# Four norms by column halves, the entries and the ending by tile, and a down projection moved behind its up projection, in a two-block transformer kernel

## The chip, the core and the metric

The kernel runs on one core of a Trainium2 chip. The metric is the device time of one execution in microseconds. One core has five engines with instruction streams of their own: TensorE (PE, matmul), VectorE (DVE), ScalarE (ACT), GpSimd (POOL) and SyncE (SP). They meet only at semaphores, and each follows its stream in order. Matmuls accumulate in eight PSUM banks of 128 x 512 fp32.

## What is computed

512 tokens of 1024 fp32 features pass through two blocks, each followed by a normalization with `final_g`. The part of the reference that matters here, cut:

```python
# block one
x = x + merged @ w_mix_out                                   # site mx
hc = rmsnorm(x, norm_cross_g); x = x + cross_attention(...)  # site co
hf = rmsnorm(x, norm_ffn_g)
x = x + peer_ffn(hf, ...)      # per token 8 heads x 16 experts of 16384:
                               # gelu(hf . u_e) * g_e * v_e, summed over the 128 chosen
x = rmsnorm(x, final_g)        # "fa"
# block two
h = rms_norm(x, ...)           # mix2
y = concat(nsa_mixer, gmlp, conv); x = x + norm(y) @ w_ou    # site ou
x = x + cross_attention(rms_norm(x), ...)                    # site xo
x = x + conv_gated_ffn(rms_norm(x), w_up, w_down)            # up, down; D_FF = 2816
return rms_norm(x, final_g)    # "fb"
```

## The kernel before

The tokens are four tiles of 128; a half `h` is two tiles (`h=0`: tiles 0 and 1, `h=1`: tiles 2 and 3). `X` holds the residual of all four. Weights come in chunks of 128 x 1024 fp32 (512 KB) through a ring of six buffers, `RING`: SP issues the chunk with number k once PE has used the one with number k-6. Each expert is one indirect gather on POOL of 1 MB (a row of u and of v for each of 128 tokens) into one of eight slots. For each of the 512 gathers DVE makes a dot product (L1951), ACT the gelu and the gate (L1446, L1450), and the gated v row is added to X either by DVE (`add` on DVE, L1928) or by PE with a diagonal matrix into PSUM (L1180), whose sum DVE adds to X in `total` (L1941).

The order of all work is a list of steps that the class `Plan` writes; every engine, the DMA issue of SP among them, works off the steps that concern it in that order. The list has three stretches:

- `first_a`: block one of tiles 0 and 1 up to the norm `("ffn", 0)`.
- the weave: `weave(work, peers, choices)` interleaves three lists by the costs written beside the steps. `peers` are the 512 experts, tile by tile; `work` holds everything else of block one of tiles 2 and 3 and then `second(0, True)`, block two of tiles 0 and 1, up to its up projection `proj_T("up", 0, 11)`. While `light` is set, two of three experts are summed on PE.
- `second(1, False)`: block two of tiles 2 and 3. It starts when the experts of tile 3 are summed (`total` 3): final norm `fa` (`final_in` loads the gain row, `final_sq`, `final_inv`, `final_root`, `final_out`), norm `mix2`, eight transposes on each tile, the projections qn, kn, vn, zg, zc, `cmp1`/`cmp2`, 20 steps of attention (`nsa`: logits "nl" L1123, transposes "nt" L1088 and L1090, values "nv" L1102 and L1108), the y norm, ou, cross attention, up and down.

The down projection of tiles 0 and 1 stands inside `second(1)` (`late_down`): it runs over the 22 chunks of w_down twice, once for each tile, and its 44 pieces are placed by `beside(n)`: 8 before the mix2 transposes, 1 or 2 behind each attention step, the rest before the y transposes. Its matmuls (`down`, L1153) need nothing of tiles 2 and 3. `last(0)` (the final norm and the store of tiles 0 and 1) stands behind the ou projection and before the norm `("x", 2, 1)`.

A norm is: squares of both tiles with a row sum on ACT (`norm_sq`, L1228), mean and reciprocal on DVE (`norm_inv`, L1601, L1603), root on ACT (`norm_root`, L1233, with the load of the function table for it), scaling of one tile on ACT and of the other on DVE (`norm_out`, L1250, L1613), then 16 transposes on PE (L897, L898), evicted by ACT and DVE (L1259, L1627). `proj_T` (L909, L910) and `proj_tok` (L929, L930) are the two forms of a projection; `out_tok` adds its result to X by column halves of 512 (`residual`, L1638).

## Time and profile before

| | us |
|---|---|
| three runs | 2905.11, 2905.76, 2908.76 (median 2905.76) |
| the profiled execution | 2902.87 |
| its span in the trace | 2901.1 |
| PE busy | 2408.7 (83%) |
| DVE busy | 1765.4 (61%) |
| ACT busy | 1124.4 (39%) |
| POOL busy | 665.2 (23%) |

The profiled execution is 2.9 us below the median of the three runs, and 1.8 us longer than its span. Times in the rows are counted from the start of the span. A share of busy time is a mean over stretches that are bounded by different things, so each stretch is read by itself.

### The profile page before, as it was taken

How to read it: one execution, taken by the hardware profiler on the slowest of the kernel's cores; microseconds unless marked ns; L12 is line 12 of the kernel's file. 1: busy time of each engine (PE TensorE's matmuls, PEld its weight loads, DVE VectorE, ACT ScalarE, POOL GpSimd, SP SyncE). 2: the span in 40 equal slices, each digit the busy share in tenths (PEclk: the TensorE clock that was granted, in tenths of full speed). 3: DMA queues.
4: the chain of work that ended last, by engine and by line, in shares of the span. 5: the costliest groups of instructions: out<-in, count | busy, mean ns of one | idle time of the engine just before them, and what ended most of it. 6: DMA issues, size and time to landing. Idle time of an engine off the chain costs nothing.

```text
span 2901.1 us, 31007 instructions
## 1 busy us (share of the span) xinstructions
PE 2408.7 (83%) x10834; PEld 1655.5 (57%) x10834; DVE 1765.4 (61%) x4230; ACT 1124.4 (39%) x2762; POOL 665.2 (23%) x569
## 2 busy tenths in 40 slices
PE   8999999879978649778958588577984799988998
PEld 7786666657744327536626434354762376655873
DVE  2101311598797778676999898888998417312430
ACT  2101311242533764354442578464554225412210
POOL 0000000122343344332233334443234102100000
PEclk9999999989989879999979566699996699999999
DMA  6555343589999999999889989999999653443443
GB/s 205 173 153 166 96 145 126 213 333 371 403 412 417 416 392 391 419 398 393 314 333 416 368 324 379 390 419 419 416 418 419 258 161 111 152 131 94 153 153 116
DMA packets 160972, 838.74 MB, mean 289 GB/s; under 512 B 17400, under 2 KB 21896, under 8 KB 95024
## 3 DMA queue, kind: packets, MB, share of 16 engines
q0 software_dynamic: 73728, 536.90, 45.8%
q1 hardware_dynamic: 82464, 287.75, 28.6%
q10 hardware_dynamic: 4624, 12.11, 1.2%
q8 instruction: 86, 1.41, 0.2%
q14 instruction: 70, 0.57, 0.1%
HBM read 828.27 MB, written 8.41 MB: 288 GB/s over the span
## 4 chain that ended last, share of the span: by engine, by line
PE 50%; DVE 22%; ACT 13%; DMA 10%; issue 4%; POOL 0%; ACTq 0%; DVEq 0%; SPq 0%
PE ps L909 24%; DMA BIG<-in_uv,BIG 9%; DVE BIG L1951 6%; PE ps L929 5%; DVE X L1928 5%; PE ps L930 5%; PE ps L1153 5%; PE ps L910 3%; ACT L1446 2%; PE ps L1180 2%; DVE BIG L1859 1%; DVE BIG L1856 1%; PE ps L1123 1%; PE ps L1102 1%; ACT WK L1228 1%
## 5 line engine op out<-in xcount | busy, mean ns | idle before, releaser
L2168 POOL DMA_INDIRECT BIG<-in_uv,BIG x512 | 622.0, 1215 | 1635.1 <-DVE X L1928 576.0
L909 PE MATMUL ps<-BIG,RING 128*128 128x256 f32 x3472 | 810.6, 386 | 15.2 <-DMA RING<-in_w_cq 4.9
L909 PEld LDWEIGHTS ps<-BIG,RING 128*128 128x128 f32 x3472 | 665.5, 193 | 148.0 <-issue 26.5
L1951 DVE CUSTOM_DVE_ANT_0 BIG<-BIG 128x1024 f32<-128x1024 f32 x512 | 619.2, 1217 | 87.1 <-DMA BIG<-in_uv,BIG 84.8
L1928 DVE SCALAR_TENSOR_TENSOR X<-BIG,small,X 128x1024 f32<-128x1024 f32 x333 | 426.3, 1280 | 75.0 <-ACT small L1450 74.3
L1446 ACT ACTIVATE small<-small 128x1 f32<-128x1 f32 x512 | 102.7, 201 | 640.5 <-DVE small L1951 636.3
L909 PE MATMUL ps<-WK,RING 128*128 128x256 f32 x1232 | 291.0, 389 | 21.3 <-DVE BIG L1707 19.3
L909 PEld LDWEIGHTS ps<-WK,RING 128*128 128x128 f32 x1232 | 238.6, 195 | 62.2 <-DVE BIG L1707 26.8
L929 PE MATMUL ps<-RING,BIG 128*128 128x512 f32 (+1 forms) x448 | 225.7, 585 | 5.6 <-DVE BIG L1686 2.4
L930 PE MATMUL ps<-RING,BIG 128*128 128x512 f32 (+1 forms) x448 | 223.5, 580 | 0.0
L1279 ACT ACTIVATE BIG<-ps 128x256 f32<-128x256 f32 (+2 forms) x143 | 56.5, 397 | 375.8 <-PE ps L910 316.7
L1180 PE MATMUL ps<-BIG,DG 64*64 64x512 f32 x728 | 131.4, 811 | 82.3 <-ACT DG L1458 82.3
L1180 PE MATMUL ps<-BIG 64*64 64x512 f32 x704 | 126.8, 811 | 54.2 <-ACT BIG L1458 54.0
L1645 DVE TENSOR_SCALAR BIG<-ps 128x256 f32<-128x256 f32 (+2 forms) x37 | 16.8, 454 | 252.1 <-PE ps L910 207.7
L1153 PE MATMUL ps<-RING,BIG 128*128 128x512 f32 x352 | 161.3, 612 | 3.1 <-DVE X L1941 3.1
L897 PE MATMUL ps<-ident,BIG 128*128 128x128 f32 x128 | 48.0, 385 | 134.9 <-ACT BIG L1250 77.9
L1446 ACT ACT_TABLE_LOAD x117 | 150.1, 1283 | 2.7 <-issue 0.6
L1638 DVE TENSOR_TENSOR X<-ps,X 128x512 f32<-128x512 f32 x40 | 27.4, 690 | 198.2 <-PE ps L930 117.9
L910 PE MATMUL ps<-BIG,RING 128*128 128x256 f32 x496 | 147.5, 379 | 0.0
L929 PEld LDWEIGHTS ps<-RING,BIG 128*128 128x128 f32 x448 | 84.1, 191 | 106.6 <-issue 93.9
L930 PEld LDWEIGHTS ps<-RING,BIG 128*128 128x128 f32 x448 | 85.6, 191 | 101.9 <-issue 100.5
L1228 ACT ACTIVATE WK<-X 128x1024 f32<-128x1024 f32 x32 | 33.8, 1056 | 222.2 <-DVE X L1638 207.2
(258 smaller groups left out, 2860.1 us busy)
## 6 DMA issues: line engine op xcount, KB each, us to landing
RING<-in_w_up SPq DMA_DIRECT2D x88, 512.0 KB
RING<-in_w_down SPq DMA_DIRECT2D x66, 512.0 KB
RING<-in_w_pq SPq DMA_DIRECT2D x32, 512.0 KB
RING<-in_w_cc SPq DMA_DIRECT2D x16, 512.0 KB
RING<-in_w_cx SPq DMA_DIRECT2D x16, 512.0 KB
RING<-in_w_cb SPq DMA_DIRECT2D x16, 512.0 KB
RING<-in_w_cv SPq DMA_DIRECT2D x16, 512.0 KB
RING<-in_w_gc SPq DMA_DIRECT2D x16, 512.0 KB
```

What stands on the lines that cost most here:

```text
L909: e.matmul(ps[:, 0:256], W[:, j, :], src[:, j, 0:256], start=j == 0, stop=False)
L910: e.matmul(ps[:, 0:256], W[:, 7, :], src[:, 7, 0:256], start=False, stop=True).then_inc(pe.sem, pe("mm", site, h, c, m))
L929: e.matmul(ps[:, 0:n], src[:, 2 * j, t * 128:(t + 1) * 128], W[:, 0, :], start=j == 0, stop=False)
L930: mm = e.matmul(ps[:, 0:n], src[:, 2 * j + 1, t * 128:(t + 1) * 128], W[:, 1, :], start=False, stop=j == 3)
L1153: mm = e.matmul(ps[:, :], AF[h][:, f, t * 128:(t + 1) * 128], W[:, hh * 512:(hh + 1) * 512], start=f == 0, stop=f == 21)
L1180: mm = e.matmul(banks[6 + half_of][to:to + 64, :], d[rows, :], v[rows, 1024 + 512 * side:1536 + 512 * side], start=first, stop=last)
L1228: e.activation(SQ[:, 0:width], src(i), ACT.Square, accum_out=small[:, o + i:o + i + 1]).then_inc(act.sem, act("sq", key, i))
L1279: e.activation(dst, ps[:, 0:dst.shape[-1]], ACT.Copy, scale=scale).then_inc(act.sem, act("ev", site, h, c, m))
L1446: e.activation(a, dots[:, k % 8:k % 8 + 1], ACT.Gelu).then_inc(act.sem, act("gelu", k))
L1928: e.scalar_tensor_tensor(out=X[:, t, :], in0=slot[slot_of[k]][:, 1024:2048], scalar=acts[:, k % 8:k % 8 + 1], in1=X[:, t, :], op0=ALU.mult ...
L1951: e.tensor_tensor_reduce(out=u, in0=HF[:, t % 2, :], in1=u, scale=1.0, scalar=0.0, op0=ALU.mult, op1=ALU.add, accum_out=dots[:, k % 8:k % ...
L2168: e.indirect_dma_start(out=slot[i], out_offset=None, in_=I["uv"], in_offset=bass.IndirectOffsetOnAxis(ap=IDX[:, t, c:c + 1], axis=0)).then ...
```

## The change

1. The norms `("x",1,0)`, `("ffn",0)`, `("x",2,1)` and `("ffn2",1)` are made by column halves: while the projection in front of them works on its second half of columns, ACT squares the first half and loads the table for the root (`quick_first`); behind it ACT squares the second half and takes the root with the first half's mean as its bias (`quick_sq`), and the scaling is in halves, so that the first four transposes wait for the first half alone.
2. The entry of tiles 2 and 3 (`fa` and `mix2`) goes tile by tile (`enter`). Tile 2's is written into the weave, behind `down(0)` and behind the total of tile 2, tile 3's at the start of `second(1)`. The gain row of `fa` for them gets a buffer of its own.
3. The down projection of tiles 0 and 1 stands in the weave, right behind their up projection, in one pass over 22 chunks with four pieces each (`down(0)`). `late_down` and its places in `second(1)` are gone.
4. `last(0)` is split: the load of its gain row stays behind ou, the rest stands behind the norm `("x", 2, 1)` and its transposes.
5. In the last down projection the last six chunks are worked off in the order both halves of tile 2, then each half of tile 3, and the final norm and the store go by tile and half.

```diff
+QUICK = {("x", 1, 0): "mx", ("ffn", 0): "co", ("x", 2, 1): "ou", ("ffn2", 1): "xo"}
...
+                    if quick:
+                        yield 0, "quick_first", quick
                 yield 3.4, "proj_tok", site, h, c, j, k
...
+        if key in QUICK:
+            for kind in ("quick_sq", "quick_inv", "quick_out"):
+                yield 0, kind, key
+            return
...
+        yield from self.proj_tok("mx", 0, 2, False, quick=("x", 1, 0))
...
+        if layer == 2 and h:
+            yield from self.last(0)
...
+        quick = None if lean else ("ffn", 0) if layer == 1 else ("ffn2", 1)
+        yield from self.proj_tok("co" if layer == 1 else "xo", h, 2, lean, quick=quick)
...
-    def late_down(self):
-
-        for i in range(2):
-            for f in range(22):
-                k = self.next_ring()
-                yield (0, "chunk", "down", f, k), (1.7, "down", 0, f, k, (i,))
-        yield (0, "mark", ("out", 0)),
+    def down(self, h):
+
+        for f in range(22):
+            k = self.next_ring()
+            yield 0, "chunk", "down", f, k
+            yield 3.4, "down", h, f, k, (0, 1, 2, 3)
+        yield 0, "mark", ("out", h)
...
-            for steps in (islice(rest, n) if h else ()):
-                yield from steps
-        yield gap, "final_in", "fa", h
-        yield gap, "final_sq", "fa", h
-        yield 0, "final_inv", "fa", h
-        yield gap, "final_root", "fa", h
-        yield gap, "final_out", "fa", h
-        yield 0, "mark", ("s2n", h)
-        yield from self.norm_steps(("mix2", h), lean)
-        yield from beside(8)
+        if h:
+            yield from self.enter(1, 0)
+            yield 0, "mark", ("s2n", h)
+        else:
+            yield gap, "final_in", "fa", h
+            yield gap, "final_sq", "fa", h
+            yield 0, "final_inv", "fa", h
+            yield gap, "final_root", "fa", h
+            yield gap, "final_out", "fa", h
+            yield 0, "mark", ("s2n", h)
+            yield from self.norm_steps(("mix2", h), lean)
...
             if step[3] in other:
                 yield (0,) + other[step[3]]
-            yield from beside(1 + step[3] % 2)
...
         yield 0, "y_scale", h
-        yield from beside(7)
         for k in range(8):
             yield (2.0 if k == 7 else 0), "trans", ("y", h), k, lean
         self.norming = False
-        yield from self.proj_tok("ou", h, 2, lean)
+        yield from self.proj_tok("ou", h, 2, lean, quick=None if lean else ("x", 2, 1))
         if h:
-            yield from self.last(0)
+            yield 0, "final_in", "fb", 0
         yield from self.cross(2, h, lean)
         yield 0, "mark", ("f", h)
         yield from self.norm(("ffn2", h), lean, 3.0)
         yield 0, "mark", ("up", h)
         yield from self.proj_T("up", h, 11, lean)
         if h:
-            for f in range(22):
+            for f in range(16):
                 k = self.next_ring()
                 yield 0, "chunk", "down", f, k
-                yield 3.4, "down", h, f, k, (0, 1)
+                yield 0, "down", h, f, k, (0, 1, 2, 3)
             yield 0, "mark", ("out", h)
-            yield from self.last(h)
+            yield 0, "final_in", "fb", h
+            ring = {f: self.next_ring() for f in range(16, 22)}
+            for f in ring:
+                yield 0, "chunk", "down", f, ring[f]
+            for qs in ((0, 1), (2,), (3,)):
+                for f in ring:
+                    yield 0, "down", h, f, ring[f], qs
+                if qs[-1] % 2:
+                    for kind in ("tail_sq", "tail_out", "tail_store"):
+                        yield 0, kind, qs[-1] // 2
+
+    def enter(self, i, gap):
+
+        for kind in ("fa", "mix2"):
+            yield gap, "enter_sq", kind, i
+            yield 0, "enter_inv", kind, i
+            yield gap, "enter_root", kind, i
+            yield gap, "enter_out", kind, i
 
...
-        for kind in ("final_in", "final_sq", "final_inv", "final_root", "final_out"):
+        for kind in ("final_sq", "final_inv", "final_root", "final_out"):
             yield 0, kind, "fb", h
         yield 0, "store", h
...
         yield from self.second(0, True)
+        yield from self.down(0)
         self.light = True
+        while "total2" not in self.reached:
+            yield "wait"
+        yield 0, "final_in", "fa", 1
+        yield from self.enter(0, 4.0)
...
+                    self.reached.add(f"total{t - 1}")
...
+        FG1 = {"fa": [at_(L[0], 1024), at_(W0 + 14848, 1024)], "fb": [at_(o + 5632, 1024) for o in L]}
...
+            def tail_store(i):
+                for hh in range(2):
+                    w.wait_ge(*at["fin", 1, i, hh])
+                    e.dma_start(out[0, (2 + i) * 128:(3 + i) * 128, 512 * hh:512 * hh + 512],
+                                OUT[1][:, i, 512 * hh:512 * hh + 512]).then_inc(stored["out"].sem, stored["out"]("out", 1, i, hh))
...
+                    w.wait_ge(*at[("nrm", key, t) + ((k // 4,) if key in QUICK else ())])
...
+            def quick_first(key):
+                site, src = QUICK[key], norm_of(key)["src"]
+                w.wait_ge(*at[{"mx": ("rec", ("o", 0)), "co": ("mm", "xt", 1, 0, 7), "ou": ("mm", "tr", ("y", 1), 7),
+                               "xo": ("mm", "xt", 2, 1, 7)}[site]])
+                for i in range(2):
+                    w.wait_ge(*at["ev", site, key[-1], 0, i])
+                    own()
+                    e.activation(SQ[:, 0:512], src[:, i, 0:512], ACT.Square, accum_out=small[:, 500 + i:501 + i]).then_inc(
+                        act.sem, act("sqa", key, i))
+                sqrt_ahead(small[:, 500:501], key)
+
+            def quick_sq(key):
+                site, src = QUICK[key], norm_of(key)["src"]
+                for i in range(2):
+                    w.wait_ge(*at["ev", site, key[-1], 1, i])
+                    own()
+                    e.activation(SQ[:, 512:1024], src[:, i, 512:1024], ACT.Square, accum_out=small[:, 502 + i:503 + i]).then_inc(
+                        act.sem, act("sqb", key, i))
+                    own()
+                    w.wait_ge(*at["nb", key])
+                    e.activation(small[:, 506 + i:507 + i], small[:, 502 + i:503 + i], ACT.Sqrt, bias=small[:, 504 + i:505 + i],
+                                 scale=1.0 / 1024).then_inc(act.sem, act("rt", key, i))
+
...
+            def enter_sq(kind, i):
+                if kind == "fa":
+                    w.wait_ge(*at["total", 2 + i])
+                    w.wait_ge(*at["mm", "up", 0, 10, 3])
+                else:
...
+            def enter_out(kind, i):
+                o = ENTER_AT[kind] + i
+                w.wait_ge(*at["ert", kind, i])
+                if kind == "fa":
+                    w.wait_ge(*at["fa", 1])
+                    e.scalar_tensor_tensor(out=X[:, 2 + i, :], in0=X[:, 2 + i, :], scalar=small[:, o:o + 1], in1=FG1["fa"][1],
+                                           op0=ALU.mult, op1=ALU.mult).then_inc(dve.sem, dve("fin1", 1, i))
+                elif i:
+                    e.tensor_scalar(TMPz[:, 1, :], X[:, 3, :], small[:, o:o + 1], None, ALU.mult).then_inc(
+                        dve.sem, dve("nrm", ("mix2", 1), 1))
```

The root and output steps of `enter` and of the tail (`enter_root`, `enter_out` on ACT, `tail_sq`, `tail_out`, `quick_out` on DVE) have the form of those shown.

How the instructions move. On SP, from the last chunk list of the weave to the xq projection of tiles 2 and 3; L760 and L789 issue weight chunks (the source's name tells the projection), L830 and L859 are the stores of tiles 0 and 1. Before:

```order
L760 DMA RING<-in_w_up 128x1024 x44
L760 DMA RING<-in_w_down 128x1024 x8
L760 DMA RING<-in_w_qn 128x1024 x4
L760 DMA RING<-in_w_kn 128x1024 x4
L760 DMA RING<-in_w_vn 128x560 x4
L760 DMA RING<-in_w_zg 128x1024 x4
L760 DMA RING<-in_w_zc 128x1024 x4
L760 DMA RING<-in_cmp_w 128x1024 x4
L760 DMA RING<-in_w_down 128x1024 x36
L760 DMA RING<-in_w_ou 128x1024 x8
L830 DMA out<-BIG 128x1024 x2
L760 DMA RING<-in_w_xq 128x1024 x8
```

And now:

```order
L789 DMA RING<-in_w_up 128x1024 x44
L789 DMA RING<-in_w_down 128x1024 x22
L789 DMA RING<-in_w_qn 128x1024 x4
L789 DMA RING<-in_w_kn 128x1024 x4
L789 DMA RING<-in_w_vn 128x560 x4
L789 DMA RING<-in_w_zg 128x1024 x4
L789 DMA RING<-in_w_zc 128x1024 x4
L789 DMA RING<-in_cmp_w 128x1024 x4
L789 DMA RING<-in_w_ou 128x1024 x8
L859 DMA out<-BIG 128x1024 x2
L789 DMA RING<-in_w_xq 128x1024 x8
```

The 44 chunks of w_down around the entry and the attention have become 22 in front of qn; the order ou, store, xq is the same.

On PE, the end of the weave: L909/L910 and L944/L945 are the up projection, L1180 the expert sums, L1153 and L1187 the down projection, L897/L898 and L932/L933 the transposes of the entry. Before:

```order
L909 MATMUL ps<-WK,RING 128x256 x7
L910 MATMUL ps<-WK,RING 128x256
L1180 MATMUL ps<-BIG,DG 64x512 x16
L1180 MATMUL ps<-BIG 64x512 x16
L1180 MATMUL ps<-BIG,DG 64x512 x16
L1180 MATMUL ps<-BIG 64x512 x16
L1180 MATMUL ps<-BIG,DG 64x512 x12
L1153 MATMUL ps<-RING,BIG 128x512 x16
L897 MATMUL ps<-ident,WK 128x128
```

And now:

```order
L944 MATMUL ps<-WK,RING 128x256 x7
L945 MATMUL ps<-WK,RING 128x256
L1187 MATMUL ps<-RING,BIG 128x512 x88
L932 MATMUL ps<-ident,WK 128x128
L933 MATMUL ps<-ident,WK 128x128
```

The sums of the last 28 experts on PE (19 of them) are gone, and all 88 pieces of the down projection stand there.

On PE, the start of the attention of tiles 2 and 3 (L1123 and L1158 are logits, L1088/L1090 and L1123/L1125 transposes of the weights, L1153 pieces of the down projection of tiles 0 and 1). Before:

```order
L1123 MATMUL ps<-BIG 128x384 x2
L1123 MATMUL ps<-BIG 128x31
L1153 MATMUL ps<-RING,BIG 128x512 x2
L1123 MATMUL ps<-BIG 128x384 x2
L1123 MATMUL ps<-BIG 128x31
L1153 MATMUL ps<-RING,BIG 128x512 x4
L1123 MATMUL ps<-BIG 128x384 x2
L1123 MATMUL ps<-BIG 128x31
L1153 MATMUL ps<-RING,BIG 128x512 x2
L1088 MATMUL ps<-ident,BIG 128x128 x6
L1090 MATMUL ps<-ident,BIG 31x128
```

And now:

```order
L1158 MATMUL ps<-BIG 128x384 x2
L1158 MATMUL ps<-BIG 128x31
L1158 MATMUL ps<-BIG 128x384 x2
L1158 MATMUL ps<-BIG 128x31
L1158 MATMUL ps<-BIG 128x384 x2
L1158 MATMUL ps<-BIG 128x31
L1123 MATMUL ps<-ident,BIG 128x128 x6
L1125 MATMUL ps<-ident,BIG 31x128
```

The down pieces between the attention steps are gone.

On DVE, the entry of tiles 2 and 3: L1941 and L2101 are the total, L1963 and L1756 the final norm's output, L1613 the scaling of mix2, L1798 the residual of the down projection. Before:

```order
L1928 SCALAR_TENSOR_TENSOR X<-BIG,small,X 128x1024
L1941 TENSOR_TENSOR X<-ps,X 64x512 x4
L1601 TENSOR_SCALAR small<-small 128x2
L1603 RECIPROCAL small<-small 128x2
L1963 SCALAR_TENSOR_TENSOR X<-X,small,BIG 128x1024 x2
L1601 TENSOR_SCALAR small<-small 128x2
L1603 RECIPROCAL small<-small 128x2
L1613 TENSOR_SCALAR WK<-X,small 128x1024
```

And now:

```order
L2101 TENSOR_TENSOR X<-ps,X 64x512 x4
L1798 TENSOR_TENSOR X<-ps,X 128x512 x4
L1747 TENSOR_SCALAR small<-small 128x1
L1749 RECIPROCAL small<-small 128x1
L1756 SCALAR_TENSOR_TENSOR X<-X,small,BIG 128x1024
L1747 TENSOR_SCALAR small<-small 128x1
L1749 RECIPROCAL small<-small 128x1
L1747 TENSOR_SCALAR small<-small 128x1
L1749 RECIPROCAL small<-small 128x1
L1756 SCALAR_TENSOR_TENSOR X<-X,small,BIG 128x1024
L1747 TENSOR_SCALAR small<-small 128x1
L1749 RECIPROCAL small<-small 128x1
```

The four residuals of tiles 0 and 1 now stand between the total and the entry, and the entry of tile 2 as well as that of tile 3 stands behind the total of tile 3.

## Rows read from the trace of the kernel before

**Rows 1.** The page's groups: line, engine, operation, count | busy us, mean ns | idle before, releaser.

```profile
L1928 DVE SCALAR_TENSOR_TENSOR X<-BIG,small,X 128x1024 f32<-128x1024 f32 x333 | 426.3, 1280 | 75.0 <-ACT small L1450 74.3
...
L1228 ACT ACTIVATE WK<-X 128x1024 f32<-128x1024 f32 x32 | 33.8, 1056 | 222.2 <-DVE X L1638 207.2
```

**Rows 2.** Timeline of the head's last norm: start, us, engine, line, operation, out<-in, count, [idle<-releaser].

```profile
518.62 0.48 PE L897 MATMUL ps<-ident,BIG 128*128 128x128 f32 x1 [5.92 <-ACT BIG L1250]
...
523.08 5.74 PE L909 MATMUL ps<-BIG,RING 128*128 128x256 f32 x14 [0.78 <-DVE BIG L1627]
```

**Rows 3.** Windows of the weave's end: us, busy by engine (instructions), PEclk, DMA share, GB/s.

```profile
2050.00:2222.00 172.00, 127.02 (x528) 104.06 (x530) 158.54 (x274) 94.70 (x189) 52.58 (x50) 0.88 1.02 418
2222.00:2283.00 61.00, 34.07 (x144) 5.08 (x136) 41.10 (x61) 18.85 (x69) 26.54 (x21) 0.56 0.95 393
```

**Rows 4.** Timeline of gathers and chunks while the up projection runs.

```profile
2169.94 0.94 POOL L2168 DMA_INDIRECT BIG<-in_uv,BIG  x1 [2.46 <-DVE X L1928]
...
2171.05 25.33 SPq L760 DMA_DIRECT2D RING<-in_w_down  x6
...
2173.71 0.94 POOL L2168 DMA_INDIRECT BIG<-in_uv,BIG  x1 [2.82 <-DVE X L1928]
```

**Rows 5.** Timeline of the last experts and of the entry of tiles 2 and 3.

```profile
2280.41 1.23 DVE L1951 CUSTOM_DVE_ANT_0 BIG<-BIG 128x1024 f32<-128x1024 f32 x1 [1.22 <-DMA BIG<-in_uv,BIG]
...
2282.86 1.23 DVE L1951 CUSTOM_DVE_ANT_0 BIG<-BIG 128x1024 f32<-128x1024 f32 x1 [1.22 <-DMA BIG<-in_uv,BIG]
...
2287.15 2.85 DVE L1941 TENSOR_TENSOR X<-ps,X 64x512 f32<-64x512 f32 x4 [1.85 <-PE ps L1180]
...
2306.96 0.27 PE L897 MATMUL ps<-ident,WK 128*128 128x128 f32 x1
```

**Rows 6.** Windows: the attention of tiles 2 and 3 in block two.

```profile
2383.00:2517.00 134.00, 132.59 (x617) 85.79 (x616) 83.72 (x390) 72.07 (x180) 23.04 (x16) 0.97 0.37 115
```

**Rows 7.** Groups by line in 2383:2517 (busy us, mean ns | idle before <-releaser).

```profile
L1153 PE MATMUL ps<-RING,BIG 128*128 128x512 f32 x112 | 54.6, 624 | 0.0
```

**Rows 8.** Timeline of TensorE: attention steps at the half and at the full clock.

```profile
1725.63 1.12 PE L1102 MATMUL ps<-BIG,WK 128*128 128x64 f32 x4 [0.57 <-DVE small L1725]
...
2383.88 3.16 PE L1123 MATMUL ps<-BIG 64*128 64x384 f32 x6
...
2396.46 1.70 PE L1123 MATMUL ps<-BIG 64*128 64x384 f32 x6
...
2406.94 1.45 PE L1102 MATMUL ps<-BIG 128*128 128x64 f32 x12
```

**Rows 9.** Windows of attention without filler: block one, block two (tiles 0, 1), cross.

```profile
320.00:330.00 10.00, 8.36 (x29) 6.38 (x30) 3.92 (x19) 6.41 (x24) 0.00 (x0) 0.50 0.00 0
1670.00:1820.00 150.00, 122.28 (x559) 60.31 (x559) 137.47 (x444) 118.29 (x334) 64.89 (x51) 0.66 0.90 351
2606.00:2626.00 20.00, 15.28 (x68) 11.07 (x68) 7.96 (x27) 7.56 (x26) 0.00 (x0) 1.00 0.00 0
```

**Rows 10.** Timeline of the y norm.

```profile
2520.96 0.63 ACT L1564 ACTIVATE WK<-BIG 128x512 f32<-128x512 f32 x1 [2.33 <-PE ps L1153]
...
2524.28 1.93 DVE L2097 TENSOR_SCALAR BIG<-BIG,small 128x512 f32<-128x512 f32 x6 [0.90 <-ACT small L1233]
...
2531.06 0.27 PE L897 MATMUL ps<-ident,BIG 128*128 128x128 f32 x1
```

**Rows 11.** Timeline from the ou projection to the xq projection.

```profile
2562.86 2.48 DVE L1963 SCALAR_TENSOR_TENSOR BIG<-X,small,BIG 128x1024 f32<-128x1024 f32 x2 [0.27 <-ACT small L1233]
2564.17 1.54 SPq L830 DMA_DIRECT2D out<-BIG  x2
...
2569.66 0.47 PE L897 MATMUL ps<-ident,BIG 128*128 128x128 f32 x1 [8.07 <-ACT BIG L1250]
...
2573.86 3.26 PE L909 MATMUL ps<-BIG,RING 128*128 128x256 f32 x14 [0.78 <-DVE BIG L1627]
```

**Rows 12.** Timeline of the ending.

```profile
2890.30 0.69 DVE L1638 TENSOR_TENSOR X<-ps,X 128x512 f32<-128x512 f32 x1 [0.17 <-PE ps L1153]
```

More of the change, by code:

```diff
@@ L153, in proj_T, with proj_tok @@
             yield (0, "out_T") + held
[L155 removed]
+    def proj_tok(self, site, h, n, lean, first=0, quick=None):
         held = None
@@ L1140, in conv_out, with down @@
                     pe.sem, pe("mm", "ct", h, c))
-            def down(h, f, k, tiles):
+            def down(h, f, k, qs):
                 W = RING[:, k % 6, :]
@@ L1145, in down @@
                 w.wait_ge(*at["upm", h, f])
-                qs = [2 * t + hh for t in tiles for hh in range(2)]
                 for q in qs:
```

100 lines of the change are left out of this document (85 added, 15 removed).

## The prediction

> **What bounds the kernel now.** I read the page's busy shares first, its costliest groups for what one instruction takes, then windows and the timeline at each edited place. PE is busy for 83% of the span, but that mean hides three regimes. At the end of the weave the DMA engines are the bound: share 1.02 and 418 GB/s from 2050 to 2222 [rows 3]. While chunks of 0.52 MB flow beside the gathers of 1.05 MB, gathers are issued 3.77 us apart (2169.94 and 2173.71) [rows 4], which is (1.05 + 0.52) / 3.77 = 417 GB/s; at the very end, with gathers alone, the dots come 2.45 us apart, each ended by its DMA [rows 5]. In the attention of tiles 2 and 3 PE is the bound: 132.6 us busy of 134 against DVE's 83.7, at a granted clock of 0.97 [rows 6]; but 54.6 us of it is the down projection of tiles 0 and 1 [rows 7]. The third regime is the chain of a norm, in which PE stands idle: 5.92 us in the head [rows 2], 8.07 us in front of xq [rows 11].
>
> **The weave's end.** The 22 chunks of the down projection now pass while gathers pass. Before, six of them did [rows 4]. Behind the 22nd, six more chunks (qn, kn) come in as the ring frees, still before the last gather: 28 against 6, so 22 x 0.524 MB = 11.5 MB more before the last dot, at 418 GB/s [rows 3] **+27.6**. Were the six of qn and kn to come later, 16 chunks give +20; the bounds are 20 and 30 (393 GB/s, the rate of the second window). PE's part there (88 pieces, 1.7 us a chunk at full and 3.4 at half clock) fits into 3.77 us a chunk and is free. In the plan the last 28 experts are now all summed on DVE: 1.22 for the dot [rows 5] and 1.28 for the sum [rows 1], 2.5 us each, under the DMA's 3.77; hidden too, and if the chunk traffic were free, DVE would just keep the old pace.
> A rule of the Trainium skill bears on it ("DMA: Bandwidth & Descriptors", section "Queues, rings and completion order"): a DMA engine takes turns between the queues that have work. By that rule the ring's queue takes its share from the gathers even though they are the urgent ones; the spacing of 3.77 against 2.45 us agrees with it.
>
> **The entry of tiles 2 and 3.** Before, 22.9 us lie between the end of the last dot (2282.86 + 1.23) and the first transpose at 2306.96 [rows 5], with eight down chunks as cover. Now DVE has the last sum 1.28 [rows 1], the total 2.85 [rows 5], four residuals of 0.69 [rows 12], and then the entries of both tiles. Tile 2's was meant to be early, but on ACT and DVE it stands behind total 3, so both run in series. For a tile: squares 1.25 (1.06 [rows 1] and the read of the row sum), mean and reciprocal 0.4, root 0.2, output 1.24 (half of 2.48 [rows 11]), and the same again for mix2; about 5 each, 10 for two, 2.8 for the last scaling and the handoffs. Sum 19.7, so -3.2. But PE has stood still, and its 16 transposes (0.21 apart at half clock, 0.11 at full) and the first projection column (5.74 us at half [rows 2], 3.26 at full [rows 11]) cost 1.7 + 2.5 = 4.2 more, the price of one cold start that I use below too. **+1.3**, with bounds of -5 (it stays warm) and +3.
>
> **The attention of tiles 2 and 3.** The 54.6 us of down pieces are gone [rows 7], leaving 78 us of PE work at the full clock, and 81 us on DVE (83.7 less four residuals). Neither overlaps perfectly with the other: each step goes logits, softmax on DVE and ACT, transposes, values. With a quarter added for these hand-overs I expect 103 us against 133.4 if the clock stays full. But the pieces taken out were the dense ones. At the half clock a set of logits takes 3.16 us instead of 1.70, and value matmuls are 0.28 us apart instead of 0.12 [rows 8]. Sixteen steps of 8.1 and 9.5 us (384 and 512 keys) and 6 us besides make 147 us, and then PE is the bound again. Which is it? Nearby stretches without dense filler [rows 9]: block one's attention fell to 0.50 though PE was busy 8.4 us of 10; the attention of tiles 0 and 1 had 0.66; cross attention with 128-row matmuls kept 1.00 at 76% busy. The steps here are of the first two's kind (64-row logits, transposes, narrow values), with rows twice as long. I take a mean granted clock of 0.80, between 0.66 and 1.00, thus full for six tenths of the time: 1 / (0.6/103 + 0.4/147) = 117 us. **-16**, with bounds of -29 (full) and +13 (half throughout).
> The Trainium skill has a rule against this edit ("TensorE: Matmul & The Clock Gate", section "HAM oscillation — how this bites in real kernels"): idle gaps between bursts bring the clock down again and again, so that every burst is cold. By it alone the term would be near its upper bound. The rows are split: two of the three stretches agree with it, the cross attention doesn't.
>
> **The y norm.** ACT's last square waited 2.33 us for the down pieces in front of it, and the transposes at 2531.06 for those behind it [rows 10]. Without them the chain itself decides: its scaling (2524.28 and 1.93 long) ends at 2523.9 instead of 2526.2, the first transpose to about 2524.4. -6.6, and a cold start of 4.2: **-2.4** (-6.6 to 0).
>
> **Norms by halves.** The idle of 5.92 us [rows 2] holds two squares, a table load, root and a whole scaling. With the first half's squares and the table under cover, what is left is a residual, one half square (0.63 [rows 10]), root, reciprocal and a half scaling, 2.6 us: -3.4. The clock had fallen in this gap (0.50 at the transposes); a shorter one may keep it, up to 4.2 more. I take half: ("ffn",0) **-5.5** (-3.4 to -7.5). ("ffn2",1) has the same gap, but only -1 for the clock: **-4.4**. ("x",1,0) already lay under the mv projection: 0.
>
> **("x",2,1) and the stores.** The quick norm and last(0)'s removal should take some 5.5 us from the gap of 8.07 [rows 11]. But SP works in order: the stores of tiles 0 and 1 stand ahead of the eight xq chunks, and they wait for a final norm that now comes behind the transposes. Two squares (2.1 [rows 1]), root, and 2.48 of output put it at 2572.5 instead of 2564; two issues of 1.54 together [rows 11], and about 2 us of landing, put the first xq matmul near 2576.1 instead of 2573.86, at half clock after the wait. 2.2 + 2.5 = **+4.7** (-6 to +6). Nothing hides this: PE has no work between the transposes and xq.
>
> **The ending.** From the last residual (2890.30) to the span's end (2901.1) are 10.8 us [rows 12]. By tile and half there remain the residual, a half square, root, reciprocal, a half output, one issue and one landing: 6.5. **-4.3** (-2 to -5.5).
>
> **The sum.** 27.6 + 1.3 - 16 - 2.4 - 5.5 - 4.4 + 4.7 - 4.3 = +1.0 against the profiled execution of 2902.87: 2903.9. That execution was 2.9 below the median of the runs, so against the median of 2905.76 it is **2906.8**. A measurement here can tell about 0.2%, 5.8 us, from no change.
>
> **The rivals.** All other terms make +17.0 before attention is counted.
> - A (mixed clock, chance 0.42): the forecast. Attention takes 112 to 128 us; time 2901 to 2918.
> - B (the clock stays full, 0.34): attention 103 to 108 us, time 2893.8 to 2899. For it: rows of 384 and 512 keys stream twice as long as block one's, and the cross attention held 1.00. If chunks also cost only 20, the time is near 2886.
> - C (slower; the clock stays low, 0.20): attention without its dense filler runs mostly at the half clock and PE is bound by its own work. At 135 us it is +19, 2924; at 147, 2936. It decides as soon as attention takes more than about 122 us, which is when the clock is full for less than half of it. For it: block one's 0.50. Against: at the half clock PE would have no gaps, and before, a PE without gaps came back from 3.16 us for a set of logits to 1.70 [rows 8]; the down pieces were in it, though.
> - D (the chunks don't cost what their bytes say, as the gathers find slack, 0.04): weave +10, time near 2889.
> That tile 2's entry doesn't come early is in the forecast; were it early, 5 us less.
>
> **Range and chances.** From B's low end with part of the chunk doubt, 2888, to C's middle, 2928: about 1 in 10 lies outside each side. Below 2900: B, D and none of A but its edge, 0.37. Above 2911.6: C and a quarter of A, 0.32. Between: 0.31.
>
> **What will show it.** In the changed profile: DMA share about 1 until a last dot some 27 us later; the four residuals and both entries between it and the transposes, about 19.7 us; the length of the attention and its granted clock, the largest doubt; the first xq matmul ended by its ring DMA; idle of about 2.6 us before the transposes of ffn and ffn2; 6.5 us from last residual to end. A weave that grows by under 20, or attention at 1.00 in 103 us, would make the forecast too high; attention over 122 us too low.

## The result and the profile after

The changed kernel takes 2917.45 us at the median of 20 runs (2909.85 to 2939.86), the kernel before 2906.28 us (20 runs, 2903.11 to 2908.76): a ratio of 1.0048, 95% interval 1.0031 to 1.0065. It is slower, and the whole interval lies above 1. Its runs also spread over 30 us; those of the kernel before spread over 6 here and over 9 and 12 in the two larger sets (15 and 28 runs) beside the experiments. The profiled execution of the changed kernel, span 2909.1 us, is one of its shortest.

Both traces are cut at the same events. All figures are differences between starts or ends of rows, and they add up to the last line.

| stretch | before | after | change |
|---|---|---|---|
| start to first gather | 557.1 | 549.7 | -7.4 |
| first gather to last dot | 1725.8 | 1754.5 | +28.7 |
| last dot to first logits of tiles 2, 3 | 101.0 | 102.8 | +1.8 |
| attention of tiles 2, 3 | 133.4 | 126.7 | -6.7 |
| end of attention to first y transpose | 13.8 | 6.8 | -7.0 |
| y transposes to end of ou | 30.5 | 34.1 | +3.6 |
| end of ou to first xq matmul | 12.3 | 15.5 | +3.2 |
| first xq matmul to the end of the span | 327.2 | 319.1 | -8.1 |
| span | 2901.1 | 2909.1 | +8.0 |

**The head.** The timeline of PE at the norm ("ffn",0) is to be held against [rows 2]; columns as there.

```profile
515.40 0.30 PE L932 MATMUL ps<-ident,BIG 128*128 128x128 f32 x1 [2.68 <-DVE BIG L1740]
...
518.11 3.26 PE L944 MATMUL ps<-BIG,RING 128*128 128x256 f32 x14 [0.78 <-DVE BIG L1787]
```

The idle time is 2.68 us instead of 5.92, and the first projection column takes 3.26 us instead of 5.74: the clock stayed full over the shorter gap (1.00 from 515 to 520, where before it was 0.50 from 518 to 523).

**The weave's end.** Windows of the changed kernel (us, busy by engine, PEclk, DMA share, GB/s), to be held against [rows 3]: down projection in the weave, and the stretch behind it.

```profile
2196.00:2279.00 83.00, 77.60 (x173) 33.36 (x172) 61.65 (x86) 19.72 (x58) 25.61 (x24) 0.93 1.02 417
2279.00:2325.00 46.00, 0.05 (x1) 0.08 (x2) 32.37 (x47) 13.13 (x36) 1.89 (x2) 0.54 0.50 201
```

And SP's chunk issues, the gathers, DVE's entry chain and the first transpose behind it (timeline), against [rows 4, 5].

```profile
2163.55 95.09 SPq L789 DMA_DIRECT2D RING<-in_w_down  x22
2261.75 10.63 SPq L789 DMA_DIRECT2D RING<-in_w_qn  x4
2275.48 3.76 SPq L789 DMA_DIRECT2D RING<-in_w_kn  x2
```

```profile
2266.13 0.94 POOL L2330 DMA_INDIRECT BIG<-in_uv,BIG  x1 [2.85 <-DVE X L2088]
2269.89 0.94 POOL L2330 DMA_INDIRECT BIG<-in_uv,BIG  x1 [2.81 <-DVE X L2088]
```

```profile
2304.14 1.22 DVE L2111 CUSTOM_DVE_ANT_0 BIG<-BIG 128x1024 f32<-128x1024 f32 x1 [0.99 <-DMA BIG<-in_uv,BIG]
...
2307.99 2.85 DVE L2101 TENSOR_TENSOR X<-ps,X 64x512 f32<-64x512 f32 x4
...
2310.87 2.48 DVE L1798 TENSOR_TENSOR X<-ps,X 128x512 f32<-128x512 f32 x4
...
2324.95 0.45 PE L932 MATMUL ps<-ident,WK 128*128 128x128 f32 x1 [46.07 <-DVE WK L1759]
```

All 28 chunks are issued before the last gather (2284.92). The DMA engines are full up to 2279, with gathers 3.76 us apart as long as chunks flow beside them. PE works through the down projection at nearly full clock and then idles for 46.07 us, while DVE sums the last experts, adds the total and four residuals, and makes two entries in series. The last dot is at 2304.14 instead of 2282.86; with the weave as long as before it would have been at 2275.4, since the head had gained 7.4.

**The attention.** Windows of the changed kernel: the whole attention, then ten microseconds each of its start (two of them), of the stretch in which PE had not one gap, and of the return of the clock. They are to be held against [rows 6].

```profile
2407.00:2533.50 126.50, 116.70 (x500) 92.06 (x500) 81.46 (x385) 70.89 (x180) 23.04 (x16) 0.65 0.02 7
2410.00:2420.00 10.00, 5.09 (x19) 3.89 (x18) 9.21 (x41) 7.34 (x18) 1.28 (x1) 0.67 0.03 13
2420.00:2430.00 10.00, 7.15 (x24) 4.80 (x23) 8.81 (x47) 7.28 (x17) 2.56 (x2) 0.50 0.00 1
2430.00:2440.00 10.00, 10.00 (x39) 8.32 (x38) 5.06 (x27) 3.14 (x11) 1.28 (x1) 0.50 0.00 0
2490.00:2500.00 10.00, 10.00 (x59) 7.71 (x59) 7.55 (x39) 5.70 (x16) 3.20 (x2) 0.96 0.00 0
```

PE is busy for 116.7 us of 126.5 although 54.6 us of work have gone [rows 7]: the granted clock is 0.65 in the mean, and 0.50 from 2430 to 2490, where PE has no gap. It does have gaps in the 20 us in front of that. DVE's 81.5 us are what they were, less four residuals.

Before, the attention began at the half clock as well, but beside the down pieces the clock came back, and was full at 2396.5 [rows 8] (windows of the kernel before):

```profile
2380.00:2390.00 10.00, 9.23 (x52) 5.49 (x50) 5.17 (x21) 5.67 (x12) 0.00 (x0) 0.50 0.46 155
2390.00:2400.00 10.00, 10.00 (x26) 4.78 (x26) 8.50 (x40) 5.33 (x12) 1.29 (x1) 0.91 0.51 152
```

**In front of xq.** SP's issues and PE's wait, against [rows 11].

```profile
2583.74 1.54 SPq L859 DMA_DIRECT2D out<-BIG  x2
2585.32 3.50 SPq L789 DMA_DIRECT2D RING<-in_w_xq  x6
```

```profile
2590.00 4.83 PE L944 MATMUL ps<-BIG,RING 128*128 128x256 f32 x14 [10.90 <-DMA RING<-in_w_xq]
```

The transposes are done by 2579.1, at full clock; then PE waits 10.90 us for the first xq chunk, which SP issues only behind the stores.

**The ending.** The last residual and the last stores, against [rows 12]:

```profile
2903.23 0.69 DVE L1798 TENSOR_TENSOR X<-ps,X 128x512 f32<-128x512 f32 x1 [4.46 <-PE ps L1187]
```

```profile
2906.02 0.99 SPq L865 DMA_DIRECT2D out<-BIG  x2
```

From the last residual to the span's end are 5.9 us, 10.8 before.

### The profile page after: what moved, and what is told of

Same layout as the page of the kernel before. It is cut to its first block, busy times and chain, and to the rows that moved or that the text cites. A ratio compares the mean times of both kernels' runs of the same rounds, so it can differ in the third digit from the quotient of the medians.

```text
span 2909.1 us, 30764 instructions
## 1 busy us (share of the span) xinstructions
PE 2414.4 (83%) x10682; PEld 1680.9 (58%) x10682; DVE 1790.0 (62%) x4265; ACT 1124.5 (39%) x2784; POOL 658.1 (23%) x569
## 4 chain that ended last, share of the span: by engine, by line
PE 49%; DVE 21%; ACT 12%; DMA 12%; issue 4%; POOL 0%; ACTq 0%; DVEq 0%; SPq 0%
PE ps L944 24%; DMA BIG<-in_uv,BIG 11%; DVE BIG L2111 6%; PE ps L964 5%; DVE X L2088 5%; PE ps L965 5%; PE ps L945 3%; PE ps L1187 3%; ACT L1552 2%; PE ps L1214 2%; DVE BIG L2019 1%; PE ps L1158 1%; PE ps L1137 1%; DVE BIG L2016 1%; ACT L1498 1%
## 5 line engine op out<-in xcount | busy, mean ns | idle before, releaser
L2330 POOL DMA_INDIRECT BIG<-in_uv,BIG x512 | 614.9, 1201 | 1659.7 <-DVE X L2088 615.4
L944 PE MATMUL ps<-BIG,RING 128*128 128x256 f32 x3472 | 814.3, 387 | 24.5 <-DMA RING<-in_w_xq 10.9
L944 PEld LDWEIGHTS ps<-BIG,RING 128*128 128x128 f32 x3472 | 667.5, 194 | 159.1 <-issue 37.8
L2088 DVE SCALAR_TENSOR_TENSOR X<-BIG,small,X 128x1024 f32<-128x1024 f32 x352 | 451.1, 1281 | 80.4 <-ACT small L1556 79.5
L944 PE MATMUL ps<-WK,RING 128*128 128x256 f32 x1232 | 288.7, 387 | 22.9 <-DVE BIG L1867 21.1
L944 PEld LDWEIGHTS ps<-WK,RING 128*128 128x128 f32 x1232 | 237.0, 194 | 63.3 <-DVE BIG L1867 28.5
L1187 PE MATMUL ps<-RING,BIG 128*128 128x512 f32 x352 | 156.9, 607 | 9.4 <-DVE BIG L1867 9.4
L932 PE MATMUL ps<-ident,BIG 128*128 128x128 f32 x128 | 45.2, 370 | 129.4 <-ACT BIG L1356 57.5
L945 PE MATMUL ps<-BIG,RING 128*128 128x256 f32 x496 | 147.5, 379 | 0.0
L964 PEld LDWEIGHTS ps<-RING,BIG 128*128 128x128 f32 x448 | 84.6, 192 | 107.3 <-issue 94.5
L965 PEld LDWEIGHTS ps<-RING,BIG 128*128 128x128 f32 x448 | 85.9, 192 | 102.6 <-issue 101.1
L1214 PE MATMUL ps<-BIG 64*64 64x512 f32 x640 | 112.3, 794 | 39.5 <-ACT BIG L1564 39.4
L1214 PE MATMUL ps<-BIG,DG 64*64 64x512 f32 x640 | 110.6, 780 | 41.6 <-ACT DG L1564 41.5
L1798 DVE TENSOR_TENSOR X<-ps,X 128x512 f32<-128x512 f32 x40 | 27.2, 689 | 183.1 <-PE ps L965 116.0
L1187 PEld LDWEIGHTS ps<-RING,BIG 128*128 128x128 f32 x352 | 67.8, 194 | 97.5 <-issue 85.6
```

The lines of the kernel that those rows point to most:

```text
L932: e.transpose(ps[:, 0:128], tmp[:, 0, k * 128:(k + 1) * 128], ident[:, :])
L944: e.matmul(ps[:, 0:256], W[:, j, :], src[:, j, 0:256], start=j == 0, stop=False)
L945: e.matmul(ps[:, 0:256], W[:, 7, :], src[:, 7, 0:256], start=False, stop=True).then_inc(pe.sem, pe("mm", site, h, c, m))
L964: e.matmul(ps[:, 0:n], src[:, 2 * j, t * 128:(t + 1) * 128], W[:, 0, :], start=j == 0, stop=False)
L965: mm = e.matmul(ps[:, 0:n], src[:, 2 * j + 1, t * 128:(t + 1) * 128], W[:, 1, :], start=False, stop=j == 3)
L1187: mm = e.matmul(ps[:, :], AF[h][:, f, t * 128:(t + 1) * 128], W[:, hh * 512:(hh + 1) * 512], start=f == 0, stop=f == 21)
```

## The experiments

Theory: the change costs twice, by the bytes of 28 chunks instead of 6 in front of the last gather and by stores ahead of the xq chunks, and its gain in the attention is eaten by the clock, since PE's remaining matmuls there don't hold it. Rivals: the weave grew for the experts now summed on DVE; the chunks of xq are late anyway; the attention is bound by its chain.

The kernels' stages (us; mean granted clock in brackets). The stages are those of the one profiled execution, the last column is of all runs. The medians of the kernel before beside these runs were 2905.59 (e1 to e4, without fill2), 2906.35 (e3_fill2, e5, e6, e8) and 2907.08 (e9, e10); its row below has that of the result. The changed kernel itself was not run again beside the experiments, so a comparison of its median with theirs is one between separate sets of runs.

| kernel | gather to last dot | attention (clock) | ou to xq | span profiled | median (lowest to highest) |
|---|---|---|---|---|---|
| before | 1725.8 | 133.4 (0.97) | 12.3 | 2901.1 | 2906.28 (2903.11 to 2908.76) |
| changed | 1754.5 | 126.7 (0.65) | 15.5 | 2909.1 | 2917.45 (2909.85 to 2939.86) |
| e1_late_down | 1726.9 | 133.5 (0.97) | 16.4 | 2894.6 | 2896.09 (2894.62 to 2896.91) |
| e2_stores | 1754.7 | 126.7 (0.65) | 5.4 | 2898.9 | 2901.04 (2899.52 to 2910.70) |
| e3_fill1 | 1754.2 | 111.7 (0.87) | 16.1 | 2891.7 | 2896.49 (2890.52 to 2905.35) |
| e3_fill2 | 1757.4 | 117.7 (0.98) | 15.9 | 2901.4 | 2909.26 (2903.09 to 2912.83) |
| e4_thin | 1727.7 | 132.0 (0.62) | 17.4 | 2894.0 | 2901.57 (2886.22 to 2911.89) |
| e5_before_no_fill | 1727.8 | 146.6 (0.57) | 12.5 | 2966.8 | 2967.83 (2958.69 to 2975.43) |
| e6_best | 1727.2 | 133.4 (0.97) | 6.2 | 2883.3 | 2884.77 (2882.19 to 2886.46) |
| e8_six_in_weave | 1729.2 | 133.8 (0.92) | 5.4 | 2872.2 | 2872.46 (2869.62 to 2874.79) |
| e9_twelve_in_weave | 1729.0 | 134.0 (0.87) | 6.9 | 2876.6 | 2878.00 (2877.32 to 2879.62) |
| e10_thirty | 1728.4 | 135.2 (0.97) | 7.0 | 2877.0 | 2877.20 (2875.96 to 2878.72) |

### The down projection back in its old places

```diff
-        yield from self.down(0)
...
+            yield from beside(8)
...
+            yield from beside(1 + step[3] % 2)
...
+        yield from beside(7)
```

> The changed kernel with the down projection of tiles 0 and 1 put back where it stood before (44 chunks, beside the entry, the attention and the y norm); norms by halves, entries by tile, the split last(0) and the ending stay changed. Theory (chunks in the weave cost their bytes, the attention without dense filler runs at the half clock): the weave is some 28 us shorter, the attention is back at about 133 us and a granted clock of 0.97, and the time is about 2888 to 2896, with a spread of a few us like that of the kernel before. Rival (the weave grew because its last experts are summed on DVE or because of the entries, not for the chunks): the last dot stays near 2300. Rival (attention is not bound by the clock): attention is longer than the changed kernel's by the 54 us of down pieces.

The last dot (start at 2278.60), and the attention's window:

```profile
2278.60 1.23 DVE L2120 CUSTOM_DVE_ANT_0 BIG<-BIG 128x1024 f32<-128x1024 f32 x1 [1.22 <-DMA BIG<-in_uv,BIG]
```

```profile
2380.00:2513.00 133.00, 131.25 (x613) 84.97 (x611) 83.09 (x386) 72.14 (x180) 23.06 (x16) 0.97 0.37 115
```

The time is 2896.09 us, at the upper end of the forecast; the ratio to before is 0.9968 (0.9957 to 0.9980), the spread 2.3 us in 7 runs. From first gather to last dot it is 1726.9 us: all of the weave's growth is gone. The attention is what it was, and the spread is small again. Tile 2's entry could now start early, and brought nothing: from the last dot to the first transpose are 23.7 us, 24.1 before, since eight down pieces stand there on PE: DVE has finished the entry at 2293.3, PE the pieces only at 2302.3.

### The stores behind the xq chunks

```diff
-        yield 0, "store", h
...
         yield from self.proj_T("cq" if layer == 1 else "xq", h, 2, lean)
+        if layer == 2 and h:
+            yield 0, "store", 0
```

> The changed kernel with the stores of tiles 0 and 1 behind the eight xq chunks in SP's order. Theory (the chunks stand behind stores that wait for a final norm): the 10.9 us that PE waits in front of xq shrink to under 1, the clock stays full there, and the time falls by 10 to 12 us against the changed kernel. Rival (the chunks would be late anyway): PE still waits 3 us or more there, and the gain is under 5.

SP's issues of this kernel:

```profile
2571.10 16.30 SPq L790 DMA_DIRECT2D RING<-in_w_xq  x4
2587.45 0.91 SPq L860 DMA_DIRECT2D out<-BIG  x2
```

The chunks are issued while ou still runs. From the end of ou to the first xq matmul are 5.4 us instead of 15.5; with the same attention as in the changed kernel's profile (126.7 us) the span is 2898.9 against 2909.1, 10.2 less. The median is 2901.04 (ratio to before 0.9994, 0.9983 to 1.0005). That is 16.4 us under the changed kernel's, more than the 10 to 12 expected; the surplus is not shown to come from the stores, as the changed kernel's runs lie over 30 us and these over 11. What the one stretch shows is that the chunks were late only for their place in the queue.

### Filler that computes nothing

```diff
+            if h:
+                yield 0, "fill", step[3]
...
+                for _ in range(1):
+                    mm = e.matmul(ps[:, :], AF[0][:, 0, 0:128], flat(AF[0][:, 0:2, :]), start=True, stop=True)
```

> The changed kernel with one matmul of 128x128 by 128x512 more behind each of the 20 attention steps of tiles 2 and 3, on data that is there, into a bank that nobody needs: 20 x 0.86 = 17 us of PE work at the full clock. Theory (the attention is slow for its clock, and dense work brings the clock back): attention takes 105 to 118 us instead of 127 although PE has more to do, at a granted clock over 0.85, and the time falls by 8 to 20 us. Rival (the attention is bound by its chain or by its own work): it takes 127 us or up to 17 more.

> As e3_fill1, with two idle matmuls of 128x128 by 128x512 behind each attention step, 34 us of PE work. Theory: the clock is nearly full (over 0.93), attention takes 108 to 118 us as PE is now bound by 78 + 34 us of work, and the spread of the runs falls under 10 us. Rival (more filler costs its own time): attention grows by 17 us over e3_fill1, to 129.

The attention's windows, with one and with two idle matmuls behind each step:

```profile
2406.30:2517.90 111.60, 110.22 (x539) 77.17 (x539) 81.34 (x385) 70.62 (x180) 23.03 (x16) 0.87 0.02 8
```

```profile
2409.00:2526.70 117.70, 115.55 (x577) 78.31 (x577) 82.07 (x385) 71.64 (x180) 23.06 (x16) 0.98 0.02 8
```

With 17 us more to do the attention takes 15 us less: 111.7 us, at a clock of 0.87 instead of 0.65, and the median falls from 2917.45 to 2896.49 (ratio to before 0.9970, 0.9959 to 0.9982). With 34 us the clock is 0.98 and PE is bound by its own work: 117.7 us. So the chain of the attention is not the bound (it fits into 111.7), PE at the half clock is. The filler also closes PE's gaps at the start (10.00 us busy of 10 from 2410 to 2430, 5.09 and 7.15 without it). Closed gaps alone do not bring the clock back, as the changed kernel ran 60 us without one at 0.50; how much of the gain is theirs no run separates. The spread is 15 and 10 us instead of 30. The median of fill2 is 13 us above that of fill1. Between the two profiled executions the difference is 9.7 us, 6.0 of it in the attention and 3.1 in the weave; the remaining 3 are in the runs without a trace.

### The chunks' bytes alone

```diff
+                if site == "down" and n not in seen:
+                    seen.add(n)
+                    src = src[:, 0:64]
```

> The changed kernel, but each of the 22 chunks of w_down for tiles 0 and 1 brings 64 of its 1024 columns; PE multiplies as before with whatever else lies in the buffer, so that only the transfer is left out. Theory (the weave's growth is the bytes of the chunks): 10.8 MB less at 418 GB/s, the last dot comes 20 to 28 us earlier, and the time falls by as much. Rival (it is the sums on DVE, or PE): the last dot comes less than 5 us earlier.

The last dot:

```profile
2278.92 1.23 DVE L2117 CUSTOM_DVE_ANT_0 BIG<-BIG 128x1024 f32<-128x1024 f32 x1 [1.32 <-DMA BIG<-in_uv,BIG]
```

First gather to last dot is 1727.7 us, 26.8 less than in the changed kernel, with the same sums on DVE and the same matmuls on PE. The bytes are the cost; the rival falls. The time, though, fell by only 15.9 us at the median. In the profiled execution (span 2894.0 us against 2909.1) the attention, still without its dense pieces, took 132.0 us at 0.62, 5.3 more than in the changed kernel's profile, and smaller differences elsewhere took 6 more. The runs lie between 2886 and 2912; that the attention varied in them, too, is likely but has no trace.

### Only the attention's filler away, in the kernel before

```diff
-            yield from beside(1 + step[3] % 2)
         yield 0, "mark", ("y", h)
...
-        yield from beside(7)
+        yield from beside(37)
```

> The kernel before with the 30 down pieces beside the attention of tiles 2 and 3 moved behind it, to the others in front of the y transposes; nothing else differs. Theory (the attention without dense filler runs mostly at the half clock): it takes 115 to 135 us instead of 133 at a granted clock of 0.55 to 0.8, the pieces add their 52 us behind it, and the time is 2945 to 2965, with a spread of over 10 us between runs. Rival (the half clock in the changed kernel came from the idle stretch and the idle DMA in front, not from the missing pieces): the attention takes 103 to 108 us at a clock over 0.9.

```profile
2383.50:2530.00 146.50, 131.83 (x500) 103.07 (x500) 81.73 (x385) 70.71 (x180) 23.04 (x16) 0.57 0.02 6
```

The attention with less work takes longer: 146.6 us against 133.4, at 0.57. The time is 2967.83 us (ratio to before 1.0207, 1.0181 to 1.0232; 4 runs). Nothing else in this kernel was changed, and PE reached the attention as in the kernel before; an idle stretch or idle DMA in front is not needed for the half clock. The spread is 17 us. The attention's length and the time were both above what I had given (135 and 2965).

### The changed kernel, two more profiles

> The changed kernel once more, for a second profile: its 20 runs lie between 2909.85 and 2939.86, and the profile shown is at the low end. Theory (the spread is the attention's clock): if this execution is over 2915, its attention is longer than 127 us by about the difference, at a clock under 0.65, and the other stretches agree within 3 us. Rival (the spread is in the weave or in front of xq): the attention takes 127 us again and the weave or the wait differs.

> The changed kernel a third time, with the same expectations as e11_again_a.

Windows of e11_again_a (its attention, ten microseconds early and ten late in it), and the attention of e12_again_b.

```profile
2408.00:2556.00 148.00, 139.16 (x498) 108.35 (x497) 81.64 (x384) 70.60 (x180) 23.04 (x16) 0.53 0.01 6
2430.00:2440.00 10.00, 10.00 (x39) 8.44 (x39) 5.08 (x26) 3.14 (x11) 1.28 (x1) 0.50 0.00 0
2530.00:2540.00 10.00, 10.00 (x35) 7.58 (x35) 3.08 (x16) 3.72 (x11) 1.60 (x1) 0.50 0.00 0
```

```profile
2407.00:2557.30 150.30, 141.30 (x500) 109.97 (x500) 81.80 (x385) 70.42 (x180) 23.02 (x16) 0.52 0.02 6
```

Both executions fell among the long ones: 2931.95 and 2932.55 us, spans 2930.2 and 2930.8 (the kernel before took 2903.83 on the same chip). Their attention takes 148.9 and 150.4 us (clock 0.54 and 0.52), 22 and 24 more than in the first profile, with the spans 21 and 22 longer. First gather to last dot is 1754.6 and 1755.8, ou to xq 15.9 in both. In the first profile the clock came back at 2490, in these two not before 2540. So what parts these three executions is the moment at which the clock comes back. That the other runs differ in the same way is likely, but they have no trace, and what sets the moment, no run here shows.

### A version that keeps the gains

e6_best is e1_late_down with the edit of e2_stores.

> The norms by halves, the entries by tile and the new ending, with the down projection of tiles 0 and 1 where it was before and the stores of tiles 0 and 1 behind the xq chunks. Theory (the two parts that cost are gone): e1_late_down less the 10.9 us wait in front of xq, 2885 to 2887, spread under 5 us. Rival (something else then ends last there): 2890 or more.

2884.77 us, ratio 0.9921 (0.9908 to 0.9935), spread 4.3 us. Ou to xq takes 6.2 us where e1_late_down took 16.4.

Three kernels then ask whether PE's idle time at the weave's end can be had without the bytes:

```diff
         yield from self.second(0, True)
+        for steps in islice(self.rest, 6):
+            yield from steps
...
+            yield from beside(1 + (step[3] % 5 == 0))
...
+                    if downs[0] == 7:
+                        w.wait_ge(*at["dot", 508])
```

> As e6_best, but six of the 44 down pieces stand right behind the up projection in the weave, on the six chunks that are in the ring there anyway; the seventh chunk waits on SP for the dot of expert 508, so that no further chunk goes beside the gathers; the attention has 24 pieces beside it instead of 30. Theory (PE has idle time in the weave's end, only the chunk's bytes cost there): the last dot stays where it is in e6_best and the attention is 10 us shorter, 2874 to 2879. Rival (the pieces delay the expert sums on PE, or the late chunk is missed in the entry): 2885 or more.

PE at the entry (timeline) in e6_best and in this kernel, and this kernel's attention window:

```profile
2284.62 16.69 PE L1197 MATMUL ps<-RING,BIG 128*128 128x512 f32 x32 [3.04 <-DVE X L2111]
2301.15 0.27 PE L942 MATMUL ps<-ident,WK 128*128 128x128 f32 x1
```

```profile
2278.79 14.00 PE L1206 MATMUL ps<-RING,BIG 128*128 128x512 f32 x32
2292.63 0.27 PE L951 MATMUL ps<-ident,WK 128*128 128x128 f32 x1
```

```profile
2369.40:2503.10 133.70, 130.45 (x593) 85.40 (x593) 83.81 (x387) 71.94 (x180) 23.04 (x16) 0.92 0.30 95
```

2872.46 us, ratio 0.9879 (0.9863 to 0.9895), the fastest kernel here, 1.5 us under the forecast, and not in the way forecast. The last dot did stay (1729.2 us behind the first gather, 1727.2 in e6_best). But the attention, with 24 pieces instead of 30, was no shorter (133.8 at 0.92), and the gain lies in the entry: the banks of the down projection are held already, so its pieces follow the last expert sum at once, where in e6_best they wait for the total (3.04 us), and they run at the full clock, 14.00 us instead of 16.7. From the last dot to the first transpose are 14.1 us instead of 23.7.

e9_twelve_in_weave differs from it in the first six chunks and in the pieces beside the attention:

```diff
+            yield (0, "chunk", "down", f, k), (3.4, "down", 0, f, k, (0, 1, 2, 3))
...
+            yield from beside(1)
```

> As e8_six_in_weave, but the six chunks that are in the ring at the weave's end are used for both tiles at once (12 pieces, four PSUM banks held from there on), and the attention has 20 pieces beside it. Theory (PE stands idle for 19 us there, and the dense filler of 34 us in the attention keeps the clock as in e3_fill2): the last dot stays, attention takes 118 to 124 us instead of 134, and the time is 2858 to 2864. Rival (the four held banks leave four for the attention's logits, transposes and values, and PE then waits for evictions): attention stays at 130 or more, and the time is 2870 or more.

```profile
2377.20:2511.10 133.90, 130.05 (x577) 85.46 (x577) 83.47 (x387) 72.31 (x180) 23.05 (x16) 0.87 0.25 79
```

And e10_thirty in the pieces beside the attention alone:

```diff
+            yield from beside(1 + step[3] % 2)
```

> As e8_six_in_weave, with 30 instead of 24 pieces beside the attention and none in front of the y transposes. Theory (in e8 the thinner filler let the clock fall for part of the attention: 0.92, and one dip): the clock is 0.95 or more and attention takes no more than 2 us longer, though PE has 10 us more to do in it; the y norm loses its cover, and the time is within 5 us of e8_six_in_weave. Rival (the filler's amount sets the attention's length and the clock does not): attention takes 10 us longer.

```profile
2373.60:2508.80 135.20, 132.77 (x613) 85.74 (x613) 83.67 (x387) 72.21 (x180) 23.04 (x16) 0.97 0.36 113
```

e9_twelve_in_weave takes 2878.00 us (0.9905, 0.9889 to 0.9922), e10_thirty 2877.20 (0.9900, 0.9884 to 0.9917). Three amounts of down pieces beside the attention, 20, 24 and 30 (34, 41 and 52 us), thus give the same 134 to 135 us: what the thinner filler saves in work it loses in clock (0.87, 0.92, 0.97). For e9 the theory falls. e3_fill2, with as much filler, one bank held and no chunks to wait for, took 117.7 us at 0.98. PE's gaps do not make the 16 us between them: they come to 3.9 us in e9_twelve_in_weave and 2.2 in e3_fill2, and busy time times clock, an estimate of the work at the full clock, is 113 us in both. The clock makes them; whether the four held banks or the chunks lowered it stays open. e10_thirty was within 5 us of e8_six_in_weave as expected, and its clock (0.97) and its attention (1.5 us longer than e8's) were as well.

## Why the prediction was right and wrong

The predicted 2906.8 us is 10.7 under the measured median; the range (2888 to 2928) holds it. But the forecast was no change (+1.0), the chances put a faster kernel first (0.37 against 0.32 for a slower one), and it is slower. By the prediction's own steps, each against the profiled execution:

- **The weave's end**, +27.6: +28.7 measured, and shown by e4_thin, and borne out by e1_late_down, to be the chunks' bytes. DVE's 28 sums were hidden, as said.
- **The entry**, +1.3 (its own terms, -3.2 and +4.2, give +1.0): the chain from the last dot to the first transpose is 20.8 us, or 19.6 from the dot's end where I had 19.7, -3.3 against before; with the cold start +1.8 up to the attention. Right, as was that tile 2's entry doesn't come early.
- **The attention**, -16: -6.7 in this profile, +15.5 and +17 in the two others. This is the step that failed, in its size and in one argument. The size: I had taken a granted clock of 0.80 as a middle between neighbours, and from it 117 us; the clock was 0.65, 0.54 and 0.52, and the attention 126.7, 148.9 and 150.4 us. The nearest rows, by kind of work, were the attentions of [rows 9] with 0.50 and 0.66, and the cross attention, which pulled the middle up, was the odd one. My upper bound of 147 us met the long executions (149 and 150) well; that 103 us hold at the full clock no run tested, as none kept the full clock without filler (e3_fill1 took 111.7 with 17 us more to do). The argument: against rival C I had set that a PE without gaps came back to the full clock in [rows 8]. That PE had the down pieces in its stream. Without them it ran without a gap at 0.50 for 60 us in one execution and over 100 in the others.
- **The y norm**, -2.4: -7.0 to the first transpose and +3.6 behind it, -3.4 together.
- **Norms by halves**, -5.5 for the head: -5.0 at the first projection and -7.4 at the first gather, since the clock stayed full. ("ffn2",1), -4.4: with the same 2.68 us of idle and warm transposes, -4.8.
- **("x",2,1) and the stores**, +4.7: +3.2, and +1.6 for the cold first column. The mechanism and its price were right; e2_stores gives the 10 us that it hides.
- **The ending**, -4.3: -4.9.

One of the rows behind the clock of 0.80 was also misread: 1670 to 1820 is no attention without filler. Matmuls of the expert sums (64 rows, 512 columns) are half of PE's 122.3 busy us in it (groups of that window):

```profile
L1180 PE MATMUL ps<-BIG,DG 64*64 64x512 f32 x144 | 31.5, 982 | 0.9 <-ACT DG L1458 0.8
L1180 PE MATMUL ps<-BIG 64*64 64x512 f32 x128 | 29.5, 1035 | 1.3 <-ACT BIG L1458 1.2
```

The clock was 0.66 with them, and PE idle for 28 us of the 150; with the 128-row pieces of [rows 7] it was 0.97, and PE idle for 1.4 of 134 [rows 6]. Whether rows or gaps make the difference, no run here shows.

All terms but the attention's sum to +14.7 by the table, where I had +17.0. The time was decided by the one term with bounds 42 us apart, in which I had chosen the middle of two kinds of evidence rather than the nearest kind. (Its lower bound, 103 us, is -30 against 133.4 and not -29, so rival B should read 1.4 us lower.) Of the 20 runs 10 are under 2918, where A ends, 4 lie between 2919 and 2924, and 6 lie between 2929 and 2940, about where C stood (2924 to 2936). So the median lies where it does by the mix of short and long executions, which nothing in the prediction gives; that it is no further off is partly luck. The mechanism of C, PE bound by its own work mostly at the half clock, held in all three traces, the short one included, and it had been given 0.20. The prediction also had no word on the spread, though the length of this stretch hangs on when the clock returns.

The Trainium skill's rule on the clock ("TensorE: Matmul & The Clock Gate", section "HAM oscillation — how this bites in real kernels") warned rightly, but its cause there is idle gaps; the trace has such gaps in front (5.09 and 7.15 us busy of 10), and then shows the half clock in a stretch of 60 us in which PE has none.

## What to carry to other kernels

Before you move dense independent matmuls out of a stretch of narrow ones, ask what holds the clock there: in this kernel the attention took 133.4 us with 54 us of real work beside it and 126.7 to 150.4 without, and 17 us of useless work brought it from 126.7 to 111.7. A place where the work of one engine is free may be a place where its data is not; here PE was idle at the weave's end and the DMA full, and in e8_six_in_weave the six pieces whose chunks lay there already were moved at a gain. When a norm and its store are moved behind other work, look at what is queued behind the store.

## What was unexpected of the hardware

At the half clock PE stayed without a gap (10.00 us busy of 10 by the profile) for 60 to over 100 us on 64-row logits, transposes and 64-column value matmuls, at 0.50 throughout. One dense 128x128 by 128x512 matmul behind each step raised the mean to 0.87 in the profiled execution, two raised it to 0.98. And the same program's attention took 126.7, 148.9 and 150.4 us in three executions that agree within 3 us up to it.
